# The prompt's two tiles of the feed-forward norm, scaled on GpSimd instead of VectorE

## The reference

```python
def rms_norm(x, g):
    xf = x.astype(F32)
    y = xf * lax.rsqrt(jnp.mean(xf * xf, axis=-1, keepdims=True) + NORM_EPS)
    return (y * g.astype(F32)).astype(x.dtype)

def expert_choice_moe(h, router_w, w_gate, w_up, w_down):
    ...
    aff = jax.nn.softmax((xt @ router_w).astype(F32), axis=-1)
    gates, idx = lax.top_k(aff.T, cap)
    xe = xt[idx]
    ...

    # in trunk, for each layer i
    h = h + expert_choice_moe(rms_norm(h, ffn_norm[i]), router_w[i], exp_w_gate[i], exp_w_up[i], exp_w_down[i])
```

## Time and profile before

| what | us |
|---|---|
| median of 3 runs | 2410.18 |
| lowest and highest | 2408.74 to 2413.55 |
| profiled execution | 2415.29 |
| its span on the engines | 2413.5 |
| TensorE busy | 2352.5 (97%) |
| VectorE busy | 1778.0 (74%) |
| ScalarE busy | 1364.0 (57%) |
| GpSimd busy | 296.7 (12%) |

### The profile page before, as it was taken

One profiled execution on the slowest core, in us unless ns is written; L12 is line 12 of the kernel. 1 busy time (PEld: TensorE's weight loads), 2 busy tenths in 40 slices (PEclk: granted clock), 3 DMA queues, 4 the chain that ended last, 5 costly groups with the idle time before them and its releaser, 6 DMA issues.

```text
span 2413.5 us, 34584 instructions
## 1 busy us (share of the span) xinstructions
PE 2352.5 (97%) x12246; PEld 1962.0 (81%) x12246; DVE 1778.0 (74%) x2041; ACT 1364.0 (57%) x1495; POOL 296.7 (12%) x357
## 2 busy tenths in 40 slices
PE   9999999999989999999999999999989999999997
PEld 8888888888778888888878888887778888888886
DVE  7565565465778888888866677766678888888864
ACT  5233233233457777777764455444357777777762
POOL 1000000000111112211111101000112211111011
PEclk9999999999999999999999999999999999999999
DMA  7323334123599999999971533332699999999941
GB/s 252 122 91 128 109 110 137 63 91 108 204 381 394 394 390 389 395 394 389 362 174 45 144 102 96 90 94 79 201 386 385 394 391 392 390 389 395 346 127 44
DMA packets 210326, 577.42 MB, mean 239 GB/s; under 512 B 23736, under 2 KB 65208, under 8 KB 210104
## 3 DMA queue, kind: packets, MB, share of 16 engines
q1 hardware_dynamic: 194264, 528.46, 58.8%
q0 software_dynamic: 15968, 47.73, 7.9%
HBM read 547.82 MB, written 30.43 MB: 240 GB/s over the span
## 4 chain that ended last, share of the span: by engine, by line
PE 91%; DVE 4%; DMA 2%; ACT 1%; issue 1%; SPq 0%; POOL 0%; DVEq 0%; POOLq 0%; ACTq 0%
PE bank L1703 44%; PE bank L1553 40%; PE bank L1476 4%; PE bank L1897 1%; PE bank L1879 1%; DMA m_x<-rows_normed,idx_t 1%; DVE d_parts L656 1%; DMA raw<-in_ple_w_gate 1%; DVE top_v L2144 0%; DVE m_at L2147 0%; DVE xt L1976 0%; PE bank L1590 0%; ACT d_parts L647 0%; PE bank L1919 0%; DMA resid<-in_x_prompt 0%
## 5 line engine op out<-in xcount | busy, mean ns | idle before, releaser
L2305 DVE TENSOR_TENSOR w_parts<-wt,w_parts 128x2048 fp32r<-128x2048 f32 x384 | 874.6, 2290 | 132.4 <-ACT w_parts L1232 125.6
L1232 ACT CAST w_parts<-wt 128x2048 fp32r<-128x2048 f32 x384 | 734.9, 1915 | 191.2 <-PE bank L1703 183.1
L1703 PE MATMUL bank<-w_parts,m_xt 128*128 128x512 f32 x2976 | 689.5, 390 | 2.1 <-ACT m_y L1290 2.1
L1703 PEld LDWEIGHTS bank<-w_parts,m_xt 128*128 128x128 f32 x2976 | 556.1, 188 | 117.6 <-issue 2.9
L1703 PE MATMUL bank<-w_parts,m_hidt 128*128 128x512 f32 x1632 | 383.5, 394 | 2.8 <-DVE m_hidt L2297 2.8
L1553 PE MATMUL bank<-d_parts,xt 128*128 128x512 f32 (+1 forms) x1872 | 381.4, 359 | 2.2 <-DVE d_parts L656 1.8
L1703 PEld LDWEIGHTS bank<-w_parts,m_hidt 128*128 128x128 f32 x1632 | 306.3, 189 | 66.6 <-issue 3.3
L1553 PEld LDWEIGHTS bank<-d_parts,xt 128*128 128x128 f32 x1872 | 312.6, 189 | 55.3 <-issue 3.0
L656 DVE TENSOR_TENSOR d_parts<-raw,d_parts 128x512 fp32r<-128x512 f32 (+1 forms) x168 | 215.6, 1296 | 107.2 <-ACT d_parts L647 106.2
L647 ACT CAST d_parts<-raw 128x512 fp32r<-128x512 f32 (+1 forms) x168 | 183.7, 1109 | 195.7 <-PE bank L1553 185.2
L1553 PE MATMUL bank<-xt,d_parts 128*128 128x512 f32 (+1 forms) x1488 | 278.2, 342 | 5.4 <-DVE d_parts L656 3.1
(11 more groups left out here) (203 smaller groups left out, 2165.4 us busy)
## 6 DMA issues: line engine op xcount, KB each, us to landing
wt<-in_exp_w_gate SPq DMA_DIRECT2D x128, 1024.0 KB, 11.6
wt<-in_exp_w_up SPq DMA_DIRECT2D x128, 1024.0 KB, 13.4
wt<-in_exp_w_down SPq DMA_DIRECT2D x128, 1024.0 KB, 11.1
raw<-in_ret_w_in SPq DMA_DIRECT2D x32, 1024.0 KB, 5.1
raw<-in_na_w_in SPq DMA_DIRECT2D x24, 1024.0 KB, 5.3
raw<-in_ret_w_in SPq DMA_DIRECT2D x32, 512.0 KB, 4.6
raw<-in_ret_w_out SPq DMA_DIRECT2D x16, 1024.0 KB, 5.1
raw<-in_ple_w_gate SPq DMA_DIRECT2D x8, 1024.0 KB, 9.2
```

Source lines behind the costliest of these rows:

```text
L1232: nc.scalar.copy(w_parts[c % RING][:, 0, :], wt[:, place // 2, place % 2 * 2048:place % 2 * 2048 + 2048])\
L1703: last = nc.tensor.matmul(b[:, :], lhs[x][:, 2 * k + j, :], w[:, part, j, f * HALF:(f + 1) * HALF], start=(k == j == 0 and x == part == 0) ...
L2305: v.tensor_tensor(w_parts[c % RING][:, 1, :], wt[:, k // 2, k % 2 * 2048:k % 2 * 2048 + 2048], w_parts[c % RING][:, 0, :].bitcast(F32), AL ...
```

## The change

GpSimd gets a function `prompt_scaled(l)`. For each of the prompt's two tiles it takes the root, multiplies the residual tile by `rstd` (a tensor by a column) and then the result by `gain` in place (two tensors), and counts `norm_rows[n]` up. It stands where the two roots stood in GpSimd's list, in both layers. VectorE's four `scaled` calls for these tiles go. All else keeps its order.

```diff
+            def prompt_scaled(l):
+
+                n = 1 + 3 * l
+                for t in GROUP_TILES[0]:
+                    root(n, t)
+                    pool.wait_ge(gain_in[n % 2], 16 * ((n + 1) // 2))
+                    pool.wait_ge(norm_rs[n], nth(n, t))
+                    chain.link(nc.gpsimd.tensor_scalar(normed(n, t), resid[:, t, :], rstd[:, t:t + 1], None, ALU.mult))
+                    nc.gpsimd.tensor_tensor(normed(n, t), normed(n, t), gain[:, n % 2, :], ALU.mult)\
+                        .then_inc(norm_rows[n], 1)
+
...
-            for t in GROUP_TILES[0]:
-                root(1, t)
+            prompt_scaled(0)
             stored_group(0, 0)
...
             for g in (1, 0):
-                for t in GROUP_TILES[g]:
-                    root(4, t)
+                if g == 0:
+                    prompt_scaled(1)
+                else:
+                    for t in GROUP_TILES[1]:
+                        root(4, t)
                 stored_group(1, g)
...
             eight_best(0, 1, 4)
-            for t in range(2):
-                scaled(1, t)
             eight_best(0, 1, 5)
             for t in range(2):
                 norm_low(1, t)
...
             eight_best(1, 1, 3)
-            scaled(4, 0)
             eight_best(1, 1, 4)
             closed(1, 1)
             eight_best(1, 1, 5)
-            scaled(4, 1)
             eight_best(1, 1, 6)
             for t in range(2):
                 norm_low(4, t)
```

## The result

The changed kernel takes 2424.61 us (median of five runs, 2422.60 to 2425.87) where the kernel before takes 2412.54 in the same comparison: 1.0050 times as long, interval 1.0038 to 1.0062. That is 12.07 us more. The forecast was 3.96 more, and 2424.61 lies outside its range. The profiled execution is 2424.84 with a span of 2423.1; against the profiled execution of before it is 9.55 longer, since that one lay 2.75 above its own median.

A forecast was written before the change was run, and what follows sets the result against it. The prediction took TensorE's chain as the bound, broken by each layer's routing up to the gather. Layer 0's 2.89, layer 1's 0.57 and the stores' 0.5 made 3.96 us on the median 2410.18: 2414.1, range 2409.0 to 2419.5.

The forecast's parts named there:

- What bounds the kernel: Whole program: TensorE holds 91% of the chain; the change counts only where the chain leaves TensorE, at each layer's routing.
- The price of the first instruction: GpSimd's multiplication of a 128x1024 tile by `rstd`: 1.3 us, bounds 1.04 and 1.62.
- s: GpSimd's time per tile for its two new instructions together: 3.5 us, bounds 2.1 and 4.7.
- the prediction's own sum: Both layers' later `idx_t` plus the stores' 0.5 us: 4s - 10.54 + 0.5, forecast as 3.96 us more.
- The formulas: How much later each routing ends: layer 0 2s - 4.11 (2.89 us), layer 1 0.57 us.
- the two branches: Layer 1's delay: s - 2.93 up to s = 3.5, 2s - 6.43 above it.
- A shift of `idx_t` moves the rest by as much: Behind each layer's routing: no expert work starts before the gather, so a delay of `idx_t` passes on whole.
- a sign of being wrong: At the gather: the forecast is wrong if its 9 to 10 us change by more than the shift of `idx_t`.
- the term for the stores: Layer 1: later stores delay SyncE's down weights, which then share the gather's time; 0.5 us, bounds 0 and 1.9.
- The clock: Rival, layer 0's routing: TensorE's clock halves while it idles between tiles; 3.9 us on top of 3.96, 2418.0; chance 0.11.
- The engines hold each other up: Rival, layer 1: GpSimd holds VectorE's round ahead of the residual, some 0.7 us; 4.7 us in all, 2414.8; chance 0.10.
- Slow GpSimd: Rival, both routings: s = 4.3, layer 0 loses 4.49 and layer 1 2.17; 7.2 us in all, 2417.3; chance 0.18.

## Why the prediction was wrong, step by step

**What bounds the kernel.** Right: only the two routings counted, and in both the path leaves TensorE where the earlier trace rows showed it.

**The price of the first instruction: the step that failed.** The prediction took 1.3 us, between 1.04 and 1.62, for the multiplication by `rstd`; it takes 2.85. The bounds came from a memset and a select of 128 columns, and the reasoning was that an instruction that reads one tensor is at least as cheap as one that reads two. On GpSimd it isn't. The second instruction was right: 2.2 forecast, 2.34 measured. So s was 5.20 in place of 3.5, and with it the prediction's own sum gives 4 x 5.20 - 10.54 + 0.5 = 10.76 us in place of 3.96; 12.07 were measured. That these two lie so near is in part luck: the sum passes on whole what layer 0 in part gave back (7.90 us at `idx_t`, 3.82 behind the experts), and it leaves out the clock. The two errors have opposite signs.

The Trainium skill (GPSIMD Engine Reference, section Performance versus the Vector engine) led to an estimate of 2.25 us for two tensors, and the row of 2.34 agrees. Its section Engine selection calls operations with one input "roughly line-rate" on GpSimd; here the rows disagree, with 2.85 us for the product alone where VectorE did product and weights in 1.24 to 1.28. A copy at 1.04 us fits that sentence, a multiplication doesn't.

**The formulas.** Right in form. With s = 5.20 they give 2 x 5.20 - 4.11 = 6.29 in layer 0 and 2 x 5.20 - 6.43 = 3.97 in layer 1; with the clock held 6.53 and 3.26 were measured. Layer 1 had been forecast at the edge of the two branches, s = 3.5, where the earlier residual pays for most of the longer work, and landed in the other, where GpSimd's own row of work ends last. Tile 0's second multiplication ended at 1735.53 there, and the root of tile 1 followed it without idle time, at 1735.61. The forecast order of the layers held at `idx_t` (7.90 against 4.53 us) and not over the whole program (layer 0 alone 4.1 by its ratio, layer 1 alone 7.5, with intervals that just overlap), which is the matter of the next step and not of s.

**A shift of `idx_t` moves the rest by as much.** Wrong in layer 0: 7.90 us at `idx_t`, 5.00 at the gathered rows, 3.82 at the end of the experts. The gather had run beside three loads of 1 MB and taken 9.06 us; later than they, it took 6.16. The prediction had looked at these loads from the one side only, as something that could lengthen the gather of layer 1; that the gather's length might change it named as a sign of being wrong. A further 0.5 us came back as the first transposes behind the gather ran at full clock (0.88 in place of 1.54 us, the first expert 4.48 later); the 0.7 after that wasn't traced. In layer 1, where the shift is passed on, the weights and `idx_t` came at the same time, and the term for the stores was 0 (11.76 against 11.81), its lower bound, in this pair of profiles. That is not so against every profile of the old layer 1: where its attention output ran at the lower clock, in the kernel with layer 0 alone changed (12.75 us), the weights went 4.40 us ahead of `idx_t` (1748.75 and 1753.15), the gather took 7.09 us, and the rows came 8.37 us behind `idx_t`. Beside that one the changed kernel's 11.76 is 3.4 us longer, past the upper bound of 1.9; how often the kernel before runs so isn't known.

**The clock.** Named as a rival with 0.11, from s = 4.3 on or earlier. It fell in both layers. In layer 0 it fell at some 664.9 (the mean of 0.93 from 664 to 665 puts it there), behind 2.87 us of idle time, 1.09 of transposes and 1.1 of idle time, so the 4.3 us that the prediction read elsewhere were not needed. Without the multiplication by `rstd` it fell behind waits of 2.30 us (layer 0) and 1.81 (layer 1). Its price in layer 0 was 1.23 us at `shifted_logits` (677.04, with filler 675.81), not 3.9: TensorE's work grew by 0.88 us at the transposes of tile 1 (1.97 for 1.09) and 1.48 at the logits (4.45 for 2.97), not by 4.6, since the clock was back before they ended. Measured over the whole program, the difference between the kernels was 12.1 us as they are and 9.7 with filler, 2.4 less, or 4.0 when the 1.61 at the attention output, which stands in one pair of profiles, is counted as clock too.

**The engines hold each other up.** Right that they do, and the price of 0.7 us in layer 1 did not show in the changed kernel: the round ahead of the residual was held for 0.78 us (1.01 in place of 0.23) and ended before the attention output did, so VectorE still waited 0.54 us for it. It did show without the `rstd` product, at some 0.75 us. The Trainium skill (SBUF — State Buffer, section Who interferes with whom) calls the ports that the two engines share an exclusive lock, and says of VectorE's two-port modes that whoever issues first holds them for the whole instruction. While GpSimd works on two tensors the rows agree with a hold of that length (L1050 above); while it multiplies a tensor by a column they don't: the held VectorE instruction ended 1.13 us after the start at 657.36, with 1.7 us of that instruction still to run. In which mode the held instruction worked no row shows.

**Slow GpSimd** at s = 4.3 was the nearest rival, with the right cause; its 7.2 us are too few, since the measured s is 5.20, past even the upper bound of 4.7.

## What to carry to other kernels

An instruction that a trace doesn't show is bounded by its own form, not by one that seems simpler or dearer: one multiplication of a tile by a value a row can cost more than a multiplication of two tiles, and writing it in the other form can be cheaper. When work moves to a slower engine, ask first what waits for it: four spared instructions gave VectorE nothing, for it stood waiting for the same tiles. A delay ahead of a DMA is passed on only as far as that DMA takes as long as before, and the other way round, bringing a transfer forward past its neighbours moves their lateness to who needs them next.

## What the runs showed of the hardware

- GpSimd on 128x1024 float32: a tensor by a column 2.85 to 2.87 us, by a constant 2.77, on 512 columns 1.56; two tensors 2.34; two tensors of which one is a broadcast column, or the same tile twice, 1.89; a copy 1.04.
- While GpSimd multiplies two tensors, a VectorE instruction of 0.23 us that reads a small tile and a column, or two small tiles, in SBUF is held to the end of it (it then lasted up to 2.26 us); while GpSimd multiplies by a column, only through its first 1.1 us. `MAX8` kept its 0.69 us beside both.
- A gather of 96 rows of 4 KB took 6.16 and 6.29 us with little beside it (6.62 in one more kernel), and 9.06 beside three loads of 1 MB.
- TensorE's clock fell to half with a wait of 1.85 us ahead of the same matmuls in seven profiles and stayed in five. What decides between the two was not found.
